# Order of the expert jobs in a mixture-of-experts stage: the two-sized, one-sized and four-sized jobs change places

## The reference

```python
logits = (ht @ w_router + b_router).astype(jnp.float32)
top_val, top_idx = lax.top_k(logits, TOP_K)          # TOP_K = 4 of 32 experts
gates = jax.nn.softmax(top_val, axis=-1)
...
def expert_block(args):
    xblk, e = args
    hg = xblk @ w_gu[e] + b_gu[e]                     # 1024 -> 2048
    x_glu, x_lin = hg[:, :D_FF_2], hg[:, D_FF_2:]
    x_glu = jnp.minimum(x_glu, SWIGLU_LIMIT)
    x_lin = jnp.clip(x_lin, -SWIGLU_LIMIT, SWIGLU_LIMIT)
    act = x_glu * jax.nn.sigmoid(SWIGLU_ALPHA * x_glu) * (x_lin + 1.0)
    return act @ w_down[e] + b_down[e]                # 1024 -> 1024
...
out = jnp.zeros((T + 1, D), y.dtype).at[tok_pad].add(y)[:T]
```

## Time and profile before

| | us |
|---|---|
| median of 3 runs | 2172.19 (2171.77 to 2172.55) |
| the profiled execution's own time | 2178.56 |
| its span, first to last instruction | 2176.7 |
| from there: the mixture's loads run back to back | from about 1260 to 2162.70 |

### The profile page before, as it was taken

How to read it: one execution, slowest core, us unless ns; L and a number is a source line. 1 busy time by engine, 2 the same in 40 slices (tenths; PEclk the granted TensorE clock), 3 DMA queues, 4 the chain that set the end, 5 groups by cost and what they waited for, 6 DMA issues and landing times.

```text
span 2176.7 us, 29861 instructions
## 1 busy us (share of the span) xinstructions
PE 2035.7 (94%) x12586; PEld 1380.6 (63%) x12586; DVE 724.7 (33%) x1372; ACT 408.3 (19%) x788; POOL 111.7 (5%) x186
## 2 busy tenths in 40 slices
PE   9999999999999999999999999977699999998975
PEld 6888788999888888998777733322243333333422
DVE  5445433775364137774344321100011111000101
ACT  4322132221042122220232410100000010000001
POOL 0123100000000000000000000100000000001000
PEclk9999999999999999999999999988899999999987
DMA  6221343346524436448433499999999999999997
GB/s 266 112 78 41 156 165 116 145 165 232 209 78 155 155 124 233 176 170 347 155 124 141 174 389 427 427 428 426 427 427 414 427 426 427 426 427 427 427 424 308
DMA packets 44589, 587.90 MB, mean 270 GB/s; under 512 B 5392, under 2 KB 5664, under 8 KB 9504
## 3 DMA queue, kind: packets, MB, share of 16 engines
q1 hardware_dynamic: 44448, 585.92, 66.1%
HBM read 584.85 MB, written 1.05 MB: 269 GB/s over the span
## 4 chain that ended last, share of the span: by engine, by line
PE 67%; DMA 28%; DVE 3%; ACT 1%; issue 1%; SPq 0%; DVEq 0%; ACTq 0%
PE pb L412 66%; DMA arena<-in_gu 8%; DMA ring<-in_gu 6%; DMA kv<-in_gu 5%; DMA arena<-in_dne 4%; DMA kv<-in_dne 3%; DMA ring<-in_dne 2%; DVE arena L314 1%; PE pb L422 1%; DVE arena L329 1%; DVE ring L314 0%; ACT arena L373 0%; DMA ring<-in_ab_small 0%; DVE xs L314 0%; DVE arena L323 0%
## 5 line engine op out<-in xcount | busy, mean ns | idle before, releaser
L412 PE MATMUL pb<-arena,ring 128*128 128x256 f32 (+3 forms) x2816 | 527.8, 350 | 7.0 <-DVE xs L314 3.9
L412 PEld LDWEIGHTS pb<-arena,ring 128*128 128x128 f32 (+2 forms) x2816 | 461.2, 191 | 65.8 <-issue 8.9
L412 PE MATMUL pb<-arena 128*128 128x128 f32 (+14 forms) x3804 | 459.3, 324 | 25.6 <-DMA arena<-in_dne 10.8
L412 PEld LDWEIGHTS pb<-arena 128*128 128x128 f32 (+5 forms) x3804 | 342.3, 162 | 126.9 <-issue 97.3
L412 PE MATMUL pb<-arena,cst 128*64 128x512 f32 (+6 forms) x1108 | 274.9, 610 | 42.0 <-DMA ring<-in_gu 26.4
L412 PE MATMUL pb<-ring,cst 128*64 128x512 f32 (+2 forms) x784 | 246.5, 626 | 8.8 <-DMA arena<-in_gu 4.2
L412 PEld LDWEIGHTS pb<-arena,cst 128*64 128x64 f32 (+4 forms) x1108 | 88.7, 140 | 195.1 <-issue 192.8
L412 PE MATMUL pb<-ring,arena 128*64 128x512 f32 (+4 forms) x640 | 171.4, 538 | 22.4 <-DMA arena<-in_dne 17.3
L321 DVE TENSOR_SCALAR arena<-pb 128x512 f32<-128x512 f32 x30 | 20.8, 692 | 460.7 <-PE pb L412 460.7
L379 ACT ACTIVATE arena<-pb 128x512 f32<-128x512 f32 (+2 forms) x146 | 72.8, 499 | 518.6 <-PE pb L422 391.6
L412 PEld LDWEIGHTS pb<-ring,cst 128*64 128x64 f32 (+2 forms) x784 | 73.7, 138 | 130.4 <-issue 130.4
(11 more groups left out here) (162 smaller groups left out, 1612.0 us busy)
## 6 DMA issues: line engine op xcount, KB each, us to landing
arena<-in_gu SPq DMA_DIRECT2D x64, 2048.0 KB, 19.4
ring<-in_gu SPq DMA_DIRECT2D x49, 2048.0 KB, 19.4
arena<-in_dne SPq DMA_DIRECT2D x30, 2048.0 KB, 19.4
ring<-in_dne SPq DMA_DIRECT2D x22, 2048.0 KB, 19.4
kv<-in_gu SPq DMA_DIRECT2D x15, 2048.0 KB, 19.5
ring<-in_up SPq DMA_DIRECT2D x14, 2048.0 KB, 8.1
kv<-in_dne SPq DMA_DIRECT2D x8, 2048.0 KB, 19.5
ring<-in_wkv SPq DMA_DIRECT2D x7, 2048.0 KB, 7.9
```

The costliest lines, as they stand in the source:

```text
L412: r = self.e.matmul(out, lhsT, rhs, start=start, stop=stop, skip_group_check=True)
```

## The change

The order of the jobs is another. The two fixed ones stay in front; then come quad, single, quad, single, and the nine pairs stand last. Nothing else is edited: the jobs at the third and the seventh place (`REST_AT`, `COUNT_AT`) still carry the same side work.

```diff
         GROUPS.update({f"w{n}": (n,) for n in range(2)})
         GROUPS.update({f"p{n}": (2 * n + 2, 2 * n + 3) for n in range(9)})
         GROUPS.update({f"q{n}": tuple(range(4 * n + 20, 4 * n + 24)) for n in range(2)})
-        JOBS = "e0 e1 p0 p1 q0 w0 p2 p3 p4 p5 p6 p7 p8 w1 q1".split()
+        JOBS = "e0 e1 q0 w0 q1 w1 p0 p1 p2 p3 p4 p5 p6 p7 p8".split()
         REST_AT, COUNT_AT = 2, 6
```

## The result

| | before | changed |
|---|---|---|
| median of 5 runs, us | 2172.18 (2169.76 to 2172.55) | 2181.5 (2180.94 to 2184.0) |
| ratio, 95% interval | | 1.0044 (1.0032 to 1.0056) |
| profiled execution, its own time | 2178.56 | 2181.3 |
| span | 2176.7 | 2179.4 |

What follows compares the result with a forecast made beforehand. Loads were taken to bound the mixture, PE what remains after the last landing. Tail terms from `gu11` complete at 2141.3 reached 2183.0 against 2176.7, +6.3 us on the median: 2178.5 us, 0.29% slower, range 2174.5 to 2181.8.

Steps and rivals of the forecast that it cites:

- the clock case: In the last job's `dn0`: the clock falls after PE stands still, adding 1.7 us, +8.0 in all; chance 0.20.
- to the start of `dn0`: Behind the last `gu11` pass: from its last matmul to the transposed activation, 3.6 us.
- to the last squares: In the last job's parts: part 3 has its squares 13.2 us after the copy of `dn0`, copies 2.99 us apart.
- `dn0`, 7.1 us as any pass of a pair at full clock: In the tail behind the last `gu11`: the last pair's `dn0` pass takes 7.1 us, ending at 2160.4.
- rival 1: The clock falls for the last `dn0`: 1.7 us more, +8.0, or +9 if the first parts were slow too; chance 0.20.
- PE's standstill at 3.6 us: Just before the last job's `dn0`: PE stands still for 3.6 us, after which the clock might fall.
- point 6 units later: Two jobs after w0: the load only just in time, landing after 7.7 us, stays so 6 units (29.4 us) later.
- The price in the prediction: In the load stream: each us that a load is issued later than 7.7 us before its turn costs one.
- Rival 2: Early stream, unit 13 or buffers of w0 or w1: it runs dry, 1 to 5 us on top, +7 to +11; chance 0.08.
- Rival 3: At the end: loads still pace it, not slower, -0.9 or -2.4 us; chance 0.11, including halved parts at +2.3.
- Rival 4: Whole kernel: PE, busy 94%, is the bound, so reordering the same work changes nothing, +0; chance 0.05.
- The sum's +6.3: At the end: the tail's terms end at 2183.0 against 2176.7, +6.3 us, added to the median for 2178.5 us.

Runs made afterwards that it cites:

- o_end: Kernel before with only the end of the change (third and fourth places kept, nine pairs last): 2181.39 us, ratio 1.0037.
- o_single: Kernel before with its last two jobs swapped to q1 w1, so that a single ends the list: 2200.28 us, ratio 1.0132.
- cut_after: Changed kernel with seven of the eight row blocks of the last job's `dn0` pass left out, all loads kept: 2177.07 us, ratio 1.0022.
- warm_after: Changed kernel with five matmuls on constants in PE's 2.3 us wait ahead of the last transposes: 2182.74 us, ratio 1.005.
- o_start: Kernel before with q0 w0 moved to the third and fourth places, its end (w1 q1) kept: 2172.35 us, ratio 0.9993.
- cut_before: Kernel before with seven of the eight row blocks of the last job's `dn0` pass left out, all loads kept: 2175.18 us, ratio 1.0008.
- b_again: Kernel before, unedited, run again for a second profile: 2177.14 us (one run).
- o_wq: Kernel before with the middle's q0 w0 turned round to w0 q0, its end kept: 2173.58 us, ratio 0.9994.

## Why the prediction was right, and where it was not

The direction and the mechanism were right: PE's chain behind the last `gu11` sets the end, and its length without the clock was forecast to 0.2 us. The likeliest time, 2178.5, was 3.0 us short of 2181.5, and the clock case, put at 0.20, is the one that came. By its own steps:

| from the landing of the last `gu11` | predicted | measured |
|---|---|---|
| its landing in the stretch, 861.1 + 4 x 4.90 | 880.7 | 881.2 |
| to the start of its pass | 1.3 | 1.4 |
| the pass | 7.1 | 7.1 |
| to the start of `dn0` | 3.6 | 3.7 |
| `dn0`, to its copy | 7.1 | 8.6 |
| to the last squares | 13.2 | 13.2 |
| to the end | 9.4 | 9.4 |
| sum behind the landing | 41.7 | 43.4 |

- **The term that was mis-sized** is "`dn0`, 7.1 us as any pass of a pair at full clock". It measured 8.6. That was rival 1, put second because two waits of 2.7 us in the trace of before had split. Such waits decide nothing either way: of the 58 of 2.6 to 2.9 us that PE has between 1400 and 2130 in the twelve traces, 32 had a low clock in the first 3 us of the work behind them (2 of 5 in the trace of before). All four traces with the 2.3 us wait at this place (changed, o_end, o_single and cut_after) show a low clock behind it, and the one in which the wait was filled with matmuls shows none. The better forecast was there: the prediction itself put PE's standstill at 3.6 us, longer than either. Measured it is 2.32 us, then 0.66 of transposes and another 0.73 of nothing. The Trainium skill (TensorE: Matmul & The Clock Gate, "Why this matters for your kernels") advises against idle gaps between bursts of matmuls; this tail agrees with it, and by it the forecast would have been 2180.2.
- **The stream** gave the other 0.5 us. At the start PE waited 8.65 us for q0's `gu01` (8.9 forecast) and caught up with nothing lost. The "point 6 units later" is in the windows as 417 GB/s from 1610 to 1700: the load for which SP had its buffer latest was issued at 1689.08 and landed 8.9 us later, 2.0 us behind its turn. The load at the same place before, issued at 1664.79, landed in its turn; 1.0 us was lost there four loads later. The price in the prediction, a us for each us that the issue comes later than 7.7 us before the turn, was too low here, unless one of the slips of the last section fell in with it: this load was issued 6.9 us before its turn, which by that price costs 0.8. In cut_after and warm_after, the same order up to there, it was issued 7.7 and 7.8 us before and lost 0.9 and 1.7. Over the whole stream the change lost 0.5 us: zero was inside its bounds and near. Single traces differ by a us there (880.0 in o_end, 882.7 in warm_after), so the 0.5 can't be given to the start alone; o_start, with the new start alone, has 0.6. Rival 2 was there as a small term, not as the case.
- **Rival 3** (loads still pace the end) fell: no wait for a load behind 2137, the last landing 20.0 us behind `gu11` (20.5 forecast), and a part of a pair takes as long as one of a quad, 2.99 us from copy to copy.
- **Rival 4** (PE the bound throughout) fell with cut_before: seven eighths of a PE pass taken out at the end of that kernel moved nothing in the stretch. And the same work took 7.7 us (o_end) or 27.7 us (o_single) longer in another order.
- **The base**. The sum's +6.3 was set against the median. In the stretch the terms give 6.3 + 0.5 + 1.7 = 8.5 us, as measured. The 0.8 us between that and 9.3 is inside the interval (7.0 to 12.2), and stays unassigned. One step of the sum is rounded 0.2 us up: 2141.3 - 9.8 + 10.9 is 2142.4, not 2142.6.

## What to carry to other kernels

In a stage that is bound by a stream of loads, write down what stands behind the last load on which the long chain of dependent work hangs: the time of that load is fixed by how many bytes are put behind it. Put the job there that has most bytes behind its last long dependence (here the quad, 39.2 us of loads, against 19.6 for the pair and 9.8 for the single), so that the loads cover the chain. The order ahead of it mattered little here, where the buffers held. And where a tail becomes a chain of short passes with waits between, count its passes at the clock they will get, not at the one of the busy stage.

## What the runs showed of the hardware

- Between 1.5 and 2.9 us the length of a single wait did not tell whether the clock fell. A pass behind a wait of 2.71 us ran at full clock (7.09 us), one behind 2.72 us did not (8.78 us), and waits of 1.55 and 1.68 us for the last part (before, b_again), with two short ones of 0.4 to 0.5 us ahead of them, had half clock behind them. Waits of 0.64 and 0.46 us in the same place (o_start, o_wq) had full clock. Behind the tail's two waits, 2.3 and 0.73 us with 0.66 of transposes between them, it was half in four of four traces. Where the pass behind it was shortened, the low clock moved to the next work.
- The same instructions ahead of the stretch took 1253.0 to 1261.4 us in the twelve traces, which hold the same loads in the same order up to there. The cause is open.
- Now and then a unit lands 5.2 to 6.5 us behind the one before in place of 4.90, though it was issued 18 us or more before, as the 20.88 us between 19.42 and 19.28 in the changed kernel's chain. Such slips of 0.3 to 1.6 us stand in all traces and may be the differences of about 1 us in the `gu11` column; what they are is open.
